# Routing of a mixture-of-experts step without TensorE's products of constants

## The reference, cut to what matters

```python
lg = xt @ router_w_group + router_b_group            # 4 groups
grp, p_grp = argmax(softmax(lg)), max(softmax(lg))
le = (xt @ router_w_expert + router_b_expert)[group grp]   # 8 experts of that group
top_l, top_i = top_k(le, 2)
wts = p_grp * softmax(top_l)
...
h = silu(xb @ w_gate[e]) * (xb @ w_up[e])            # rows xb of expert e
y[tok] += (h @ w_down[e]) * w
```

## The kernel before, in words

| call | products | stands between |
|---|---|---|
| L1440 | 6 | the wait for `r_dve` and the last tile's transposes |
| L1442 | 1 | these transposes and the last router product |
| L1445 | 3 | that router product and the counts |
| L1463 | 10 | the counts and L1468, ahead of the wait for `oh_dve` |
| L1521 | 6 | L1468 and `slot_tables`, ahead of the wait for `wt_rdy` |
| L1568 | 2 | `slot_tables` and `rows_in(0)`, ahead of the wait for the gather |

## Time and profile before

### The profile page before, as it was taken

How to read it: one execution, slowest core, us unless ns; L and a number is a source line. 1 busy time by engine, 2 the same in 40 slices (tenths; PEclk the granted TensorE clock), 3 DMA queues, 4 the chain that set the end, 5 groups by cost and what they waited for, 6 DMA issues and landing times.

```text
span 1724.0 us, 22514 instructions
## 1 busy us (share of the span) xinstructions
PE 1657.2 (96%) x9293; PEld 1015.9 (59%) x9294; DVE 657.7 (38%) x1382; ACT 348.0 (20%) x679; POOL 163.5 (9%) x169
## 2 busy tenths in 40 slices
PE   8999999999999999999999999999999999999990
PEld 5556777777777666666688555554444444444440
DVE  1446454545542323232577654621121212121225
ACT  1113232223231222212212011111111111111115
POOL 1000000000003321121000000011111111111110
PEclk9999999999999999999899999999999999999995
DMA  7200121211017554342362522578999999999975
GB/s 228 61 21 20 50 62 50 59 53 50 23 64 209 190 170 142 123 158 88 128 218 75 210 104 79 202 302 327 374 394 375 393 397 386 386 390 391 390 289 202
DMA packets 104410, 337.67 MB, mean 196 GB/s; under 512 B 24378, under 2 KB 68482, under 8 KB 87924
## 3 DMA queue, kind: packets, MB, share of 16 engines
q1 hardware_dynamic: 89572, 276.22, 42.4%
q0 software_dynamic: 13568, 55.78, 10.7%
q10 hardware_dynamic: 1168, 4.23, 0.6%
HBM read 307.90 MB, written 35.51 MB: 199 GB/s over the span
## 4 chain that ended last, share of the span: by engine, by line
PE 91%; DMA 5%; DVE 2%; issue 1%; ACT 1%; SPq 0%; POOL 0%; DVEq 0%; POOLq 0%; ACTq 0%
PE psum L1058 12%; PE psum L1172 10%; PE psum L1478 8%; PE psum L1483 7%; PE psum L1360 6%; PE psum L1375 5%; PE psum L1510 4%; PE psum L1504 4%; PE psum L1099 4%; PE psum L962 3%; PE psum L1211 3%; PE psum L1072 2%; DMA arena<-in_w_up 2%; PE psum L1117 2%; PE psum L1491 2%; PE psum L1106 2%
## 5 line engine op out<-in xcount | busy, mean ns | idle before, releaser
L1058 PE MATMUL psum<-arena 128*128 128x258 f32 x896 | 215.3, 384 | 0.0
L1172 PE MATMUL psum<-arena 128*128 128x344 f32 x576 | 182.3, 458 | 0.0
L1058 PEld LDWEIGHTS psum<-arena 128*128 128x128 f32 x896 | 162.8, 190 | 27.9 <-issue 7.0
L1483 PE MATMUL psum<-arena 128*64 128x512 f32 x320 | 141.6, 595 | 0.7 <-ACT arena L1809 0.7
L1484 PE MATMUL psum<-arena 128*64 128x512 f32 x320 | 141.6, 595 | 0.0
L1478 PE MATMUL psum<-arena 128*128 128x512 f32 x320 | 139.8, 595 | 0.2 <-DVE arena L2559 0.2
L1172 PEld LDWEIGHTS psum<-arena 128*128 128x128 f32 x576 | 103.2, 190 | 53.0 <-issue 11.2
L1478 PEld LDWEIGHTS psum<-arena 128*128 128x128 f32 x320 | 60.0, 190 | 72.6 <-issue 72.1
L1360 PE MATMUL psum<-arena 128*128 128x258 f32 x448 | 99.7, 387 | 0.9 <-ACT arena L1766 0.9
L1375 PE MATMUL psum<-arena 128*128 128x512 f32 x224 | 99.2, 595 | 0.0
L1360 PEld LDWEIGHTS psum<-arena 128*128 128x128 f32 x448 | 86.5, 193 | 14.2 <-issue 1.3
(11 more groups left out here) (391 smaller groups left out, 2147.8 us busy)
## 6 DMA issues: line engine op xcount, KB each, us to landing
arena<-in_w_gate SPq DMA_DIRECT2D x32, 2048.0 KB, 20.6
arena<-in_w_up SPq DMA_DIRECT2D x32, 2048.0 KB, 26.3
arena<-in_w_down SPq DMA_DIRECT2D x32, 2048.0 KB, 32.6
arena<-in_w_in SPq DMA_DIRECT2D x33, 512.0 KB, 4.9
gates<-arena SPq DMA_DIRECT2D x16, 516.0 KB, 6.0
arena<-gates SPq DMA_DIRECT2D x16, 516.0 KB, 6.4
arena<-in_x_prompt SPq DMA_DIRECT2D x16, 512.0 KB, 4.6
arena<-in_w_o SPq DMA_DIRECT2D x1, 4096.0 KB, 17.0
```

Source lines behind the costliest of these rows:

```text
L1058: ins = mm(psum[:, BANK[name[0]], 0:QT], held, moved, start=(k == 0 and name in ("X1", "V6", "Y5")), stop=(k == 3), skip_group_check=True)
L1172: ins = mm(psum[:, FB + t, 0:SP3], wring[:, u, k, :], xT[:, k, t * SP3:(t + 1) * SP3], start=(k == 0), stop=(k == KD - 1))
L1483: g = mm(psum[0:64, 2, :], xgT[:, xpar, k, 0:64], wg[:, k, :], start=(k == 0), stop=(k == KD - 1))
```

## The change

All six calls of `keep_busy` and the function itself are left out. No other instruction is changed, moved or added, on any engine.

```diff
-            def keep_busy(n, bank):
-
-                for _ in range(n):
-                    mm(psum[:, bank, 0:3 * P], ident, at(Z4, 3 * P), start=True, stop=True)
...
             pe.wait_ge(r_dve, NT - 1)
-            keep_busy(6, 2)
             turn_h(NT - 1)
-            keep_busy(1, 2)
             router(NT - 1)
 
-            keep_busy(3, 2)
             pe.wait_ge(sel_dve, NT)
...
             mm(psum[:, 5, 0:NE + 1], more_w[0:NE], tri[0:NE, 0:NE + 1], start=True, stop=True).then_inc(pos_done, 1)
 
-            keep_busy(10, 2)
             for n in range(2 * NT):
...
             def slot_tables():
 
-                keep_busy(6, 6)
                 pe.wait_ge(wt_rdy, 1)
...
             slot_tables()
-            keep_busy(2, 6)
             rows_in(0)
```

## The result

The changed kernel takes 1738.54 us (median of 5 runs, 1737.08 to 1743.64) against 1730.67 us (5 runs, 1725.63 to 1732.63). The medians differ by 7.9 us. The ratio, which is not that of the two medians, is 1.006, with a 95% interval of 1.0043 to 1.0077: 7 to 13 us slower, most likely about 10. The forecast was 3.0 us more, 1731.6 us and "the same". The measured median lies inside the stated range, but it is above the 1737.2 us from which the prediction called a change slower, and the case that came is rival S.

The account below looks back on a forecast made before the run. TensorE was taken to bound the routing, constants buying its clock only in part. L1468 ending 4.3 us later and L1525 taking 6.6 us put L1473 3.0 us later: 1728.6 + 3.0 = 1731.6 us, range 1724.5 to 1739.5.

Parts of the forecast that it names:

- rival S: L1525 and expert 0: half clock lasts into the experts; +7.2 us, up to +8.8; chance 0.33.
- the ten: Constant products ahead of the first table L1468, claimed to be in its way for 1.8 us.
- the six: Constant products ahead of the slot tables L1525, claimed to be in their way for 2.0 us.
- a shift at the first expert: Weight stream starts from TensorE's progress, so a shift there passes to the end one for one, in both directions.
- the two last products: Constant products ahead of the first expert's row transposes L1473, claimed to be in their way for 1.3 us.
- Steps 1 to 4: Half clock in routing: transposes +0.5, router +1.6, counts +1.9, together +4.0; first table L1468 ends 4.3 us later.
- The price of half clock: Small routing products: 0.118 us each at full clock, 0.221 at half, taken as +0.10 us per record.
- Step 5: Slot tables L1525: clock comes back inside them after 5 us, so they take 6.6 us, to 1137.8.
- Step 6: First expert's row transposes L1473 start at 1137.9 instead of 1134.92, +3.0 us; everything behind at full clock.
- The second fall: Upper end of S: the wait behind expert 0 meets low clock, expert 1's first products pay +1.6 us, sum +8.8.
- G: Routing: clock does not matter, only order; L1473 starts 3.2 us sooner, 1725.4 us; chance 0.12.
- N: Wait for weights of 4.24 us at 1604 absorbs the 3 us delay; 1728.6 us; chance 0.10.

Follow-up runs that it names:

- e4: Kernel before without the ten constant products ahead of the first table L1468, the other 18 kept; 1730.30 us against 1729.20, ratio 1.0001.
- e5: Kernel before without the two constant products between the slot tables and the first expert's rows; 1730.39 us against 1729.35, ratio 1.0006.
- e3: Kernel before with only the last two calls kept, six products ahead of the slot tables and two behind; 1734.41 us against 1729.20, ratio 1.0034.
- e2: Kernel before with only the first three calls kept (6, 1 and 3 products, up to the counts); 1734.22 us against 1729.20, ratio 1.0031.
- e9_weights: Kernel before plus seven constant products ahead of the 28th expert's wait for its up matrix; 1727.32 us against 1728.54, ratio 0.9988.
- e1_small: Kernel before with each 384-column constant product replaced by three of 8 columns, all six calls kept; 1751.22 us against 1729.20, ratio 1.0126.
- e8_mid: Kernel before plus six constant products at the end of the cache attention; 1732.29 us against 1729.35, ratio 1.0015.
- e7_wide: Kernel before plus three constant products among the counts and L1468's products widened to 96 columns; 1728.56 us against 1729.35, ratio 0.9993.

## Why the prediction was wrong

**What bounds.** Right in its main parts: the clock is what the constants buy, they bought it only in part, the ten and the six stand in the way (e4: the ten for 1.7 us, foreseen 1.8), and a shift at the first expert reaches the end. One part was wrong: the two last products were not in the way by 1.3 us. I compared them with the gather alone and did not look at the engine that copies the rows, which still had the slot tables to do (e5).

**Steps 1 to 4.** Right. Transposes +0.7 (foreseen 0.5), router to its end +2.3 (2.1), first table could start +4.2 later (27.1 against the 23.0 of e4; foreseen 4.0), its end +4.7 (35.2 against 30.5 before; foreseen 4.3). The price of half clock was 0.22 to 0.24 us a record, as in the earlier trace rows. The rule of the Trainium skill that was weighed there, a weight load without a term for the clock (TensorE: Matmul & The Clock Gate, section LDWEIGHTS), would have left the tables as they were; the chain shows 8.12 and 8.70 us, and the earlier trace rows had been right to decide against it.

**Step 5 failed.** "I expect L1525 to count as work and the clock to come back inside it." It did not: 36 records at half clock from beginning to end, 8.70 us instead of my 6.6. The inference was from holding to rising: L1525 had held a full clock, and I took it to raise a low one too. The runs show both sides of the same instructions, 4.68 us behind constants (e3, e4) and 8.70 without (changed kernel, e2). All rises seen in the routing and in expert 0 came within runs of products with 384 or 512 columns.

**Step 6 followed.** The rows' transposes began 47.9 us behind the last output product instead of the forecast 45.3, and expert 0 was at half clock for its first 4.5 us, which I had in S and not in the sum.

**Rivals.** S is what happened, with its place and its order of cost: priced at 7.2 us, up to 8.8; measured 9.1 at expert 0's end and 10.5 at the end of the program. Its terms, each a difference to the kernel before: L1473 +5.5 (foreseen 4.2; the slot tables took 8.70 instead of 7.9, and the start was 0.5 later), the first gate product +6.8 (5.1), the dense work at half +2.3 (2.1). The second fall, at the wait behind expert 0, did not come; the clock was back at 1151.4. Its price of 1.6 us was right, but not its condition: it came in e3_last, e4_no_ten and e9_weights (1.7 us), where expert 0 had run at full clock. Given 0.33, it should have had more than the forecast, which rested on one untested inference. G fell with the first 51 us at half clock. N fell with the pause of the weight stream, which moved with TensorE, and the wait for weights was longer (4.68 us) and not shorter.

**The size.** From the forecast's +3.0 to the measured +10.5: 2.5 at L1473, of which 2.1 is the slot tables' 8.70 us instead of 6.6; 1.3 because the two last products had been hidden; 2.3 for the dense products at half clock; 1.4 behind expert 0, where I had nothing.

## What to carry to other kernels

Where constants keep TensorE's clock up, ask of each group what it stands in front of and what clock the work behind it needs; a fall is paid by all that follows until the clock is back. Here the dearest pieces stand far behind the first gap: 4.0 us in the slot tables and 2.3 in the first dense products. That an instruction has held the clock is no evidence that it brings it back. When a filler is taken away, look at every engine between it and the next product, not only at the transfer that it seems to wait for.

## What the runs showed of the hardware that was not expected

- The same 18 products of L1525 run at a full clock from beginning to end (4.7 us in before, e3_last and e4_no_ten), and at a half clock from beginning to end (8.7 us in the changed kernel, e1_small and e2_first).
- Products with 128 columns of weights and only three columns to multiply pay for the low clock: 36 records took 8.1 us at half clock, and 4.64 us in e8_mid, where the clock was full for all but the last half microsecond. In e7_wide they had 96 columns each and took 4.75 us at full clock, so 32 times the columns cost about 0.1 us there.
- The stretches at half clock move between executions of equal code: 10 to 17 us at the end of the cache attention, none or 6.7 us in the counts (e8_mid, before), and none or about 3 us behind expert 0 (before, e9_weights; 1.7 us lost). By these rows the time moves by some microseconds from this alone, an estimate; that this is what scatters the runs was not shown.
